# Prompt attention on one core: a stepped order, probabilities turned before they are divided by their sums

## The chip, the cores and the metric

One core of one Trainium2 chip. The metric is the device time of one execution in microseconds (us), as a median of several runs. A core has five engines that run side by side and wait for one another through semaphores: TensorE (PE, matmuls and transposes, its weight loads listed as PEld), VectorE (DVE), ScalarE (ACT), GpSimd (POOL), and SyncE (SP), which issues the DMA transfers here. SBUF is the working memory; PSUM, in banks of 128 x 512 float32, is where TensorE writes. GpSimd works on SBUF alone in this kernel.

## The reference

The program is one inference step of a two-layer trunk on 1024 prompt tokens and 8 x 8 sample tokens: an RWKV-7 layer, then a layer of sliding-window attention, each with a SiLU gate and an output projection. The part at stake is the prompt's attention of the second layer: 8 tiles of 128 queries, 16 heads of 64 in 4 groups that share keys and values, a window of 128, so each tile sees two blocks of 128 keys (the first tile one). All is float32.

```python
def window_attend(q, k, v, q_pos, k_pos, sinks):
    s = jnp.einsum('bnqhgd,bnshd->bnhgqs', q, k) * ATT_SCALE
    dist = q_pos[:, :, None] - k_pos[:, None, :]
    s = s - alibi_slopes()[None, None, :, :, None, None] * dist
    s = jnp.where(live, s, NEG)              # live: 0 <= dist < WINDOW
    p = softmax(concatenate([s, sink], -1))[..., :-1]
    return jnp.einsum('bnhgqs,bnshd->bnqhgd', p, v)

o = window_attend(...)                       # (tokens, 1024)
out = (o * silu(gate)) @ w_out
```

## The kernel before

The program runs its stages one after the other: mixed projections, the delta rule, a first output projection with layer norm, the attention's projections with the sample attention, the prompt attention (`attention`, L1862 on), and a second output projection with layer norm (`out2`, matmuls at L1434). A barrier stands between the last two, and the second needs all of `o`, the gated attention output. The order on each engine inside `attention` is written out by hand: each engine has its own loop over tiles `t` and head groups `g` and waits on counting semaphores.

For a group of four heads (`t`, `g`):
- TensorE `scores` (L1954) multiplies queries and keys into one of two PSUM tiles `sc`, two heads to a bank.
- VectorE `bias_group` (L2032) scales, adds the bias table and takes the maximum of each row (L2041, one operation a head), then makes `low`, the negative of the larger of maximum and sink, in two small operations (L2047, L2049), and `extra`, the sink less that maximum (L2051).
- ScalarE `raise_group` (L2005) takes the exponential in place with its row sum (L2009, one a head, each followed by a read of the accumulator), then that of `extra` (L2012).
- VectorE `norm_group` (L2053) adds `extra` to the sums and takes the reciprocal.
- GpSimd multiplies the probabilities of each head by the reciprocal of its sum (L1936), 128 x 256 at a time.
- TensorE `turn_probs` (L1942) transposes them into the two banks of `turn`, bank `s` for key block `s`; ScalarE `keep_probs` (L1997) copies both banks to `prob_t` in SBUF.
- TensorE `values` (L1964) multiplies values and probabilities of two groups into the PSUM tile `pv`, the two groups on the two halves of the partitions.
- VectorE `gate_group` (L2060) multiplies `pv` by the gate into `o`, four multiplies of 64 x 256 for two groups.

Scores and exponentials of tile `t` are mixed with the transposes and values of tile `t - 1`. At the end of each tile TensorE also transposes the values of the tile (L1988), through the first `turn` bank, and ScalarE copies them (L2023). SyncE loads for each tile `q_in`, the keys (four transfers, eight for tiles 4 and 7, whose preceding block is loaded again), `v_in` and `gate`; the load of tile `t`'s gate waits for the gating of tile `t - 2`, and the next tile's loads stand behind it.

Of the kernel before, what the change touches and what calls it, by code (L numbers as in the profile page):

```python
# [16 lines left out]
ALU = mybir.AluOpType  # L17
# [4 lines left out]
DT = D // 128  # L22
SEQ, NB, NT = 1024, 8, 8
N = SEQ + NB * NT
TILES = SEQ // 128
# [1836 lines left out]
def attention(nc, group, a, scr, outp, o, tables, o_sample, ahead):  # L1862
# [3 lines left out]

    with Tensors(nc, "att", group) as m:

        q_in, keys = m.sb("q_in", 128, 2, DT, 128), m.sb("keys", 128, KVH, 4 * 128)
        v_in, gate = m.sb("v_in", 128, 2, 2, 128), m.sb("gate", 128, 2, DT, 128)  # L1870
        v_rows = m.sb("v_rows", 128, 2, 256)
# [4 lines left out]
        top, low, sums, extra = (m.sb(x, 128, H) for x in ("top", "low", "sums", "extra"))  # L1876
# [6 lines left out]
        v_turned, v_kept = m.sem("v_turned"), m.sem("v_kept")  # L1883
        scored, biased, topped, lowered, sunk = (m.sem(x) for x in ("scored", "biased", "topped", "lowered", "sunk"))
        raised, totalled, inverted, normed = (m.sem(x) for x in ("raised", "totalled", "inverted", "normed"))
        p_turned, p_kept, mixed, gated = (m.sem(x) for x in ("p_turned", "p_kept", "mixed", "gated"))
# [11 lines left out]
        PLACE = (0, 1, 2, 3, 1, 2, 3, 1)  # L1898

        with nc.Block() as block:  # L1900
            @block.sync
            def _(sp):
# [27 lines left out]
            @block.gpsimd  # L1930
            def _(pool):
                for t in range(TILES):
                    for g in range(KVH):
                        pool.wait_ge(inverted, 4 * t + g + 1)
                        for h in range(4 * g, 4 * g + 4):
                            pool.tensor_scalar(score[:, t % 2, h, 0:width(t)], score[:, t % 2, h, 0:width(t)], sums[:, h:h + 1], None, ALU.mult).then_inc(normed, 1)  # L1936

            @block.tensor
            def _(pe):
                pe.wait_ge(small_loaded, 32)  # L1940

                def turn_probs(b, g):  # L1942

                    pe.wait_ge(normed, 16 * b + 4 * g + 4)
                    if b or g:
                        pe.wait_ge(p_kept, 4 * b + g)
                    if g == 0:
                        pe.wait_ge(v_kept, b + 1)
                    for s in range(len(blocks(b))):
                        for h in range(4):  # L1950
                            mm = pe.transpose(turn[:, s, 128 * h:128 * h + 128], score[:, b % 2, 4 * g + h, 128 * s:128 * s + 128], ident[:])
                    mm.then_inc(p_turned, 1)
# [11 lines left out]
                def values(b, i):  # L1964
                    pe.wait_ge(p_kept, 4 * b + 2 * i + 2)
                    if b:
                        pe.wait_ge(gated, 8 * (b - 1) + 4 * i + 4)
                    for s, k in enumerate(blocks(b)):
                        for e in range(2):
                            g = 2 * i + e  # L1970
                            mm = pe.matmul(pv[64 * e:64 * e + 64, i, :], v_rows[:, k % 2, 64 * g:64 * g + 64], prob_t[:, g, s, :],
                                           start=s == 0, stop=k == b)
                    mm.then_inc(mixed, 1)

                for t in range(TILES):
                    pe.wait_ge(loaded[t % 2], 32 * (t // 2 + 1))
                    pe.wait_ge(keys_loaded[t % 2], 64 * sum(2 if u and PLACE[u] <= PLACE[u - 1] else 1 for u in range(t % 2, t + 1, 2)))
                    for g in range(KVH):
                        if t:
                            turn_probs(t - 1, g)  # L1980
                        scores(t, g)
                        if t and g % 2:
                            values(t - 1, g // 2)
                    if t:

                        pe.wait_ge(p_kept, 4 * t)
                    for j in range(2):
                        mm = pe.transpose(turn[:, 0, 128 * j:128 * j + 128], v_in[:, t % 2, j, :], ident[:])  # L1988
                    mm.then_inc(v_turned, 1)
                for g in range(KVH):  # L1990
                    turn_probs(TILES - 1, g)
                    if g % 2:
                        values(TILES - 1, g // 2)

            @block.scalar
            def _(act):
                def keep_probs(b, g):  # L1997
                    act.wait_ge(p_turned, 4 * b + g + 1)
                    if b:
                        act.wait_ge(mixed, 2 * (b - 1) + g // 2 + 1)  # L2000
                    for s in range(len(blocks(b))):
                        keep = act.activation(prob_t[:, g, s, :], turn[:, s, :], ACT.Copy)
                    keep.then_inc(p_kept, 1)

                def raise_group(t, g):  # L2005

                    act.wait_ge(lowered, 4 * t + g + 1)
                    for h in range(4 * g, 4 * g + 4):
# [267 lines left out]
```

## Time and profile before

| | us |
|---|---|
| median of 3 runs | 1588.14 |
| lowest and highest | 1587.09, 1591.98 |
| the profiled execution, its own time | 1592.97 |
| its span | 1591.2 |
| prompt attention in it | 1337.1 to 1477.1 |
| second output projection in it | 1477.1 to 1591.2 |

The profile is one execution recorded by the hardware. "Busy" is the time in which an engine has at least one instruction under way; PE's matmuls overlap one another and their ends are modelled, so PE's busy time says less than the distance from one start to the next. PEclk is the granted TensorE clock as a share of 2.4 GHz; 0.50 is 1.2 GHz. A name such as `att_turn` is the program's tile `turn` of stage `att`.

### The profile page before, as it was taken

The page shows a single profiled execution, that of the slowest core. Times are in us where ns is not written, and L with a number is a line of the kernel's source. Part 1 is how long each engine was busy: PE and PEld are TensorE (multiplying, and loading weights), DVE is VectorE, ACT ScalarE, POOL GpSimd, SP SyncE. Part 2 cuts the span into 40 slices and gives each one's busy share as a digit, 9 for nine tenths or more (in the row PEclk, how much of TensorE's full clock was granted, in tenths as well). Part 3 has the DMA queues.
Part 4 walks back from the last instruction along what each step waited for, and adds up shares of the span by engine and source line. Part 5 has one row for each costly group of instructions (what it writes and reads, how often), then busy time and mean ns, then how long its engine had stood idle before and what let it go on. Part 6 is the DMA issues. An engine that isn't in the chain of part 4 may idle for free. (4 is left out here: it accounts for less than half of the span.)

```text
span 1591.2 us, 39091 instructions
## 1 busy us (share of the span) xinstructions
PE 1462.3 (92%) x16960; PEld 1305.3 (82%) x16960; DVE 821.4 (52%) x1662; ACT 594.1 (37%) x1207; POOL 307.5 (19%) x344
## 2 busy tenths in 40 slices
PE   5999999999699499999999978999999997887897
PEld 5989898888599499999999946889999995544686
DVE  6636345777610257776677544471111122886446
ACT  7526347777511022122221314251111132786424
POOL 0000000000000244455444420000001001997000
PEclk9999999999899699999999988999999998999899
DMA  6523222556541653345334127206334344331202
GB/s 219 180 61 91 83 96 88 174 174 212 156 135 43 141 134 72 82 96 149 87 73 90 37 67 260 79 1 204 85 82 120 83 125 130 124 98 39 81 27 86
DMA packets 242379, 173.56 MB, mean 109 GB/s; under 512 B 148607, under 2 KB 218175, under 8 KB 241039
## 3 DMA queue, kind: packets, MB, share of 16 engines
q1 hardware_dynamic: 209063, 155.56, 33.8%
q10 hardware_dynamic: 33152, 15.60, 3.3%
q8 instruction: 129, 2.11, 0.5%
q14 instruction: 35, 0.29, 0.1%
HBM read 110.97 MB, written 60.46 MB: 108 GB/s over the span
## 5 line engine op out<-in xcount | busy, mean ns | idle before, releaser
L329 PE MATMUL mix_acc<-mix_high,mix_w_high 128*128 128x364 f32 (+1 forms) x768 | 181.6, 345 | 19.4 <-DVE mix_w_low L543 13.9
L329 PE MATMUL mix_acc<-mix_low,mix_w_high 128*128 128x364 f32 (+1 forms) x768 | 172.0, 333 | 4.3 <-DVE mix_low L529 4.1
L329 PE MATMUL mix_acc<-mix_high,mix_w_low 128*128 128x364 f32 (+1 forms) x768 | 171.5, 332 | 0.0
L329 PEld LDWEIGHTS mix_acc<-mix_high,mix_w_high 128*128 128x128 f32 x768 | 132.2, 191 | 40.9 <-issue 20.7
L329 PEld LDWEIGHTS mix_acc<-mix_low,mix_w_high 128*128 128x128 f32 x768 | 134.6, 191 | 6.4 <-DVE mix_low L529 6.4
L329 PEld LDWEIGHTS mix_acc<-mix_high,mix_w_low 128*128 128x128 f32 x768 | 135.6, 191 | 0.0
L1936 POOL TENSOR_SCALAR att_score<-att_score,att_sums 128x256 f32<-128x256 f32 (+1 forms) x128 | 110.3, 882 | 119.4 <-DVE att_sums L2058 119.4
L543 DVE TENSOR_TENSOR mix_w_low<-mix_wt,mix_w_high 128x1024 fp32r<-128x1024 f32 x32 | 39.2, 1225 | 135.0 <-ACT mix_w_high L391 134.7
L1328 PE MATMUL out_acc<-qkvg_room_r_high,qkvg_room_w_high 128*128 128x364 f32 (+1 forms) x320 | 105.8, 331 | 3.0 <-issue 1.9
L1328 PE MATMUL out_acc<-qkvg_room_r_low,qkvg_room_w_high 128*128 128x364 f32 (+1 forms) x320 | 105.2, 329 | 0.0
L1328 PE MATMUL out_acc<-qkvg_room_r_high,qkvg_room_w_low 128*128 128x364 f32 (+1 forms) x320 | 105.2, 329 | 0.0
L405 ACT ACTIVATE mix_out<-mix_acc 128x364 f32<-128x364 f32 (+1 forms) x96 | 38.4, 473 | 168.9 <-PE mix_acc L329 168.8
L1638 DVE CAST qkvg_room_w_high<-qkvg_room_wt 128x1024 fp32r<-128x1024 f32 x20 | 14.0, 699 | 154.4 <-DMA qkvg_room_wt<-in_w_att 154.4
L925 PE MATMUL delta_gram<-delta_kr,delta_bk 64*64 64x128 f32 x1088 | 73.1, 282 | 21.9 <-DMA delta_seq_mask<-in_seq_mask 17.2
L1143 ACT ACTIVATE delta_lm<-delta_lm 128x128 f32<-128x128 f32 x96 | 26.5, 276 | 171.9 <-PE delta_lm L960 169.6
L925 PEld LDWEIGHTS delta_gram<-delta_kr,delta_bk 64*64 64x64 f32 x1088 | 62.9, 140 | 23.4 <-DMA delta_seq_mask<-in_seq_mask 17.5
L253 POOL MEMSET mix_decay<- 128x16 f32 x8 | 1.0, 128 | 395.6 <-ACT mix_decay L459 395.6
L524 DVE SCALAR_TENSOR_TENSOR early_xs<-early_xpad,mix_rest_mu,early_xs 128x1024 f32<-128x1024 f32 x96 | 68.7, 777 | 6.8 <-ACT early_xs L369 6.8
L1238 DVE TENSOR_TENSOR delta_inv<-delta_inv,delta_grown 128x256 f32<-128x256 f32 (+1 forms) x96 | 36.0, 375 | 68.4 <-PE delta_grown L975 68.4
L1203 DVE TENSOR_TENSOR delta_grams<-delta_gram,delta_gram_mask 128x512 f32<-128x512 f32 x68 | 44.6, 674 | 45.1 <-PE delta_gram L925 45.1
L2009 ACT ACTIVATE att_score<-att_score,att_low 128x256 f32<-128x256 f32 (+1 forms) x128 | 61.5, 487 | 8.9 <-DVE att_low L2049 8.7
L1685 ACT ACTIVATE qkvg_room_out<-out_acc 128x364 f32<-128x364 f32 (+1 forms) x40 | 18.7, 474 | 120.6 <-PE out_acc L1328 120.6
(253 smaller groups left out, 3495.8 us busy)
## 6 DMA issues: line engine op xcount, KB each, us to landing
mix_wt<-in_w_in SPq DMA_DIRECT2D x32, 512.0 KB, 4.1
qkvg_room_wt<-in_w_att SPq DMA_DIRECT2D x20, 512.0 KB, 4.1
delta_bk<-scr_bk SPq DMA_DIRECT2D x17, 512.0 KB, 4.6
delta_kr<-scr_kr SPq DMA_DIRECT2D x17, 512.0 KB, 7.0
scr_kr<-mix_outs SPq DMA_DIRECT2D x16, 512.0 KB, 3.5
scr_bk<-mix_outs SPq DMA_DIRECT2D x16, 512.0 KB, 4.4
early_xpad<-in_xpad SPq DMA_DIRECT2D x8, 548.5 KB, 8.2
scr_xg<-early_xs SPq DMA_DIRECT2D x8, 544.0 KB, 2.7
```

Source lines behind the costliest of these rows:

```text
L329: mm = pe.matmul(acc[:, s, k, 0:width], w[:, s, d, :], r[:, d, n0:n0 + width], start=d == 0 and q == 0, stop=d == DT - 1 and q == 2)
L405: act.activation(out[:, s, n0:n0 + width], acc[:, s, k, 0:width], ACT.Silu if n >= G_ * DT else ACT.Copy).then_inc(evacuated, 1)
L524: dve.scalar_tensor_tensor(o[k], x[k], rest_mu[:, place, d:d + 1], o[k], ALU.mult, ALU.add).then_inc(mixed, 1)
L543: dve.tensor_tensor(w_low[:, n % 2], wt[:, n % 2], w_high[:, n % 2].bitcast(F32), ALU.subtract).then_inc(w_split, 1)
L925: mm = pe.matmul(gram_bank[n % 2][p, 256 * j + 128 * k:256 * j + 128 * k + 128], bk[p, c % 2, k, pair, :], kr[p, c % 4, :, pair, :], start ...
L1143: act.activation(blocks(lm[:, lev, 4 * g:4 * g + 4, :].rearrange("p j n -> p (j n)"), lev, 0), lm_bank[g][:, 0:128].rearrange("p (m b) -> ...
L1203: dve.tensor_tensor(grams[:, c % 3, 2 * n:2 * n + 2], gram_bank[n % 2][:, :].rearrange("p (j k n) -> p j k n", j=2, k=4), mask, ALU.mult). ...
L1238: dve.tensor_tensor(dst, dst, src, ALU.add).then_inc(grown_kept, 1)
L1328: mm = pe.matmul(out, w[:, d, :], r[:, d, columns], start=d == 0 and k == 0, stop=d == DT - 1 and k == 2)
L1685: act.activation(out[:, s, n0:n0 + n], banks[s][k][:, 0:n], ACT.Silu if name == "ag" else ACT.Copy).then_inc(evacuated, 1)
L1936: pool.tensor_scalar(score[:, t % 2, h, 0:width(t)], score[:, t % 2, h, 0:width(t)], sums[:, h:h + 1], None, ALU.mult).then_inc(normed, 1)
L2009: act.activation(score[:, t % 2, h, 0:width(t)], score[:, t % 2, h, 0:width(t)], ACT.Exp, bias=low[:, h:h + 1], accum_out=sums[:, h:h + 1] ...
```

## The change

The order becomes steps. `STEPS` counts `n` from -1 to 36; group `n` is tile `n // 4`, head group `n % 4`, and in step `n` each engine does its part for a fixed lag: TensorE the scores of group `n + 1`, the transposes of group `n - 3` and, in odd steps, the values of a pair of groups; VectorE the bias of group `n`, the reciprocal of group `n - 2`; ScalarE the exponentials of group `n - 1` and the evacuation of group `n - 3`.

The probabilities are no longer divided by their sums. Instead the reciprocals are spread: in even steps GpSimd copies those of 8 heads 64 times each into `wide` (128 x 512), as the first thing in its step, TensorE transposes `wide` into a `turn` bank (`spread_sums`), and VectorE multiplies the gate by it in place (`scale_gate`). `gate_half` then multiplies `pv` and gate in one 128 x 512 operation for two groups; for this `values` writes pairs of heads to the two partition halves, by 256 columns. GpSimd also adds the sink terms. VectorE evacuates the second block of odd groups (`by_vector`). The `turn` banks are used in the order of the list `USES`, alternating. All values are loaded in one transfer and transposed in step 2.

```diff
+        USES = [("values", k) for k in range(TILES // 2)]
+        for tile in range(TILES):
+            for group4 in range(KVH):
+                if group4 % 2 == 1:
+                    USES.append(("sums", tile, group4 // 2))
+                USES += [("probs", tile, group4, part) for part in range(len(blocks(tile)))]
+        def by_vector(b, g, s):
+            return g % 2 == 1 and s == 1
+        def turn_bank(*use):
+            return turn[:, USES.index(use) % 2, :]
+        STEPS = range(-1, GROUPS + 5)
...
             @block.sync
                     if t >= 2:
                         sp.wait_ge(scored, 4 * (t - 1))
-                        sp.wait_ge(v_turned, t - 1)
...
-                    sp.dma_start(v_in[:, slot], scr["av"][t]).then_inc(loaded[slot], 16)
+                    if t == 0:
+                        sp.dma_start(v_in[:], scr["av"][0:TILES].rearrange("t p j n -> p t j n")).then_inc(v_loaded, 16)
                     if t >= 2:
-                        sp.wait_ge(gated, 8 * (t - 1))
+                        sp.wait_ge(gated, 2 * (t - 1))
                     sp.dma_start(gate[:, slot], scr["ag"][t]).then_inc(gate_loaded[slot], 16)
...
             @block.gpsimd
-                            pool.tensor_scalar(score[:, t % 2, h, 0:width(t)], score[:, t % 2, h, 0:width(t)], sums[:, h:h + 1], None, ALU.mult).then_inc(normed, 1)
+                pool.tensor_scalar(less_sink[:], sink[:], -1.0, None, ALU.mult).then_inc(sink_turned, 1)
...
+                    pool.wait_ge(lowered, n + 1)
+                    pool.tensor_tensor(extra[:, hs], low[:, hs], sink[:, hs], ALU.add).then_inc(sunk, 1)
...
+                    pool.wait_ge(raised, 5 * n + 5)
+                    pool.tensor_tensor(total, total, extra[:, 4 * g:4 * g + 4], ALU.add).then_inc(totalled, 1)
...
+                def widen(b, i):
+                    pool.wait_ge(inverted, 4 * b + 2 * i + 2)
+                    if b:
+                        pool.wait_ge(spread, 2 * (b - 1) + i + 1)
+                    rows = sums[:, b % 2, 8 * i:8 * i + 8].rearrange("p (h o) -> p h o", o=1).broadcast_to([128, 8, 64])
+                    pool.tensor_copy(wide[:, i, :].rearrange("p (h n) -> p h n", h=8), rows).then_inc(widened, 1)
+                for n in STEPS:
+                    if live(n - 3) and n % 2 == 0:
+                        widen((n - 3) // 4, (n - 3) % 4 // 2)
+                    if live(n):
+                        add_sink(n)
+                    if live(n - 1):
+                        total_sums(n - 1)
...
             @block.tensor
+                def spread_sums(b, i):
+                    pe.wait_ge(widened, 2 * b + i + 1)
+                    wait_for_bank("sums", b, i)
+                    for j in range(4):
+                        mm = pe.transpose(turn_bank("sums", b, i)[:, 128 * j:128 * j + 128], wide[:, i, 128 * j:128 * j + 128], ident[:])
+                    mm.then_inc(spread, 1)
...
+                    for g in (2 * i, 2 * i + 1):
+                        for s, k in enumerate(blocks(b)):
+                            probs = prob_t[:, g, s, :].rearrange("p (j h n) -> p h j n", j=2, h=2)
+                            for h in range(2):
+                                at = 256 * (g % 2)
+                                mm = pe.matmul(pv[64 * h:64 * h + 64, i, at:at + 256], v_rows[:, k, 64 * g:64 * g + 64], probs[:, h], start=s == 0, stop=k == b)
...
+                for n in STEPS:
+                    if live(n + 1):
+                        scores(t, (n + 1) % 4)
+                    if n == 2:
+                        pe.wait_ge(v_loaded, 16)
+                        for k in range(TILES // 2):
+                            turn_values(k)
+                    if live(n - 5) and n % 2 == 1:
+                        values((n - 5) // 4, (n - 5) % 4 // 2)
+                    if live(n - 3):
+                        if n % 2 == 0:
+                            spread_sums((n - 3) // 4, (n - 3) % 4 // 2)
+                        turn_probs((n - 3) // 4, (n - 3) % 4)
...
             @block.scalar
+                for n in STEPS:
+                    if live(n - 1):
+                        raise_group((n - 1) // 4, (n - 1) % 4)
+                    if n == 2:
+                        for k in range(TILES // 2):
+                            act.wait_ge(v_turned, k + 1)
+                            act.activation(v_rows[:, 2 * k:2 * k + 2, :].rearrange("p t n -> p (t n)"), turn_bank("values", k), ACT.Copy).then_inc(v_kept, 1)
+                    if live(n - 3):
+                        keep_probs((n - 3) // 4, (n - 3) % 4)
...
             @block.vector
+                    dve.scalar_tensor_tensor(low[:, hs], top[:, hs], -1.0, less_sink[:, hs], ALU.mult, ALU.min).then_inc(lowered, 1)
...
+                for n in STEPS:
+                    if live(n):
+                        bias_group(n // 4, n % 4)
+                    if live(n - 2):
+                        invert_sums(n - 2)
+                    if live(n - 3) and n % 2 == 0:
+                        scale_gate((n - 3) // 4, (n - 3) % 4 // 2)
+                        if n - 3 >= KVH:
+                            keep_probs((n - 3) // 4, (n - 3) % 4)
+                    if live(n - 5) and n % 2 == 1:
+                        gate_half((n - 5) // 4, (n - 5) % 4 // 2)
```

`wait_for_bank` waits until the use of `turn` two places back in `USES` has been read: by ScalarE for values and most blocks, by VectorE for sums (`gate_scaled`) and the blocks of `by_vector` (`p_kept_too`). `keep_probs` (VectorE) is the copy of such a block to `prob_t`.

## Rows read from the trace of the kernel before

**Rows 1.** Stretches: length, busy PE PEld DVE ACT POOL (count), PEclk, DMA, GB/s.
```profile
1342.50:1356.10 13.60, 10.31 (x60) 7.29 (x60) 8.79 (x62) 8.10 (x39) 8.56 (x15) 0.54 1.00 351
...
1401.40:1416.60 15.20, 12.65 (x84) 7.35 (x82) 13.50 (x60) 12.61 (x46) 14.60 (x17) 1.00 0.33 101
...
1459.20:1477.10 17.90, 11.05 (x40) 4.86 (x40) 3.72 (x10) 4.30 (x9) 5.96 (x7) 0.71 0.00 0
1477.10:1591.20 114.10, 102.22 (x432) 82.54 (x432) 57.51 (x79) 42.15 (x71) 0.10 (x1) 0.94 0.18 68
```

**Rows 2.** Waits, 1325 to 1480: total us, times, longest.
```profile
POOL att_score L1936 <- DVE att_sums L2058: 119.4, 11, 112.1
...
PEld att_turn L1951 <- POOL att_score L1936: 19.1, 21, 2.2
```

**Rows 3.** Timeline, steady part: start, length, engine, line, op, count [idle before].
```profile
1408.68 14.41 POOL L1936 TENSOR_SCALAR att_score<-att_score,att_sums 128x256 f32<-128x256 f32 x16 [0.60 <-DVE att_sums L2058]
...
1408.68 1.94 PE L1971 MATMUL att_pv<-att_prob_t,att_v_rows 128*64 128x512 f32 x8 [0.79 <-ACT att_prob_t L2002]
...
1410.55 0.44 PE L1988 MATMUL att_turn<-all_ident,att_v_in 128*128 128x128 f32 x2
...
1411.56 1.07 PE L1951 MATMUL att_turn<-all_ident,att_score 128*128 128x128 f32 x8 [0.57 <-ACT att_v_rows L2023]
...
1412.55 1.14 PE L1960 MATMUL att_sc<-att_keys,att_q_in 64*128 64x256 f32 x8
...
1413.90 0.42 DVE L2041 CUSTOM_DVE_ANT_0 att_score<-att_sc,all_bias 128x256 f32<-128x256 f32 x1
...
1415.41 0.16 DVE L2047 TENSOR_TENSOR att_low<-att_top,all_sink 128x4 f32<-128x4 f32 x1
...
1415.67 1.08 ACT L2002 ACTIVATE att_prob_t<-att_turn 128x512 f32<-128x512 f32 x2 [1.25 <-PE att_turn L1951]
...
1416.64 0.51 ACT L2009 ACTIVATE att_score<-att_score,att_low 128x256 f32<-128x256 f32 x1
...
1417.13 0.50 ACT L2009 ACTIVATE att_score<-att_score,att_low 128x256 f32<-128x256 f32 x1
...
1425.83 0.44 PE L1988 MATMUL att_turn<-all_ident,att_v_in 128*128 128x128 f32 x2
```

**Rows 4.** Timeline, change from tile 0 to tile 1.
```profile
1350.91 0.71 PEld L1951 LDWEIGHTS att_turn<-all_ident,att_score 128*128 128x128 f32 x4 [3.12 <-issue]
...
1356.12 0.51 ACT L2009 ACTIVATE att_score<-att_score,att_low 128x256 f32<-128x256 f32 x1 [0.41 <-DVE att_low L2049]
```

**Rows 5.** Groups by shape, GpSimd and VectorE: count | busy, mean ns | idle before.
```profile
L902 POOL TENSOR_TENSOR delta_below<-delta_grams,delta_level_mask 128x512 f32<-128x512 f32 x48 | 59.6, 1270 | 0.0
...
L1203 DVE TENSOR_TENSOR delta_grams<-delta_gram,delta_gram_mask 128x512 f32<-128x512 f32 x68 | 44.6, 674 | 45.1 <-PE delta_gram L925 45.1
...
L551 DVE COPY early_v_tokens<-mix_acc 128x512 f32<-128x512 f32 x16 | 10.3, 685 | 23.4 <-PE mix_acc L267 23.4
```

**Rows 6.** Two small VectorE lines: count, ns least/median/most, first and last start.
```profile
L2047 DVE TENSOR_TENSOR att_low<-att_top,all_sink x32: 161/163/553, 1344.9 to 1455.6; 128x4 f32<-128x4 f32 x32
...
L2049 DVE TENSOR_SCALAR att_low<-att_low x32: 169/354/508, 1345.1 to 1455.8; 128x4 f32<-128x4 f32 x32
```

**Rows 7.** Timeline, end of prompt attention.
```profile
1459.09 0.19 ACT L2012 ACTIVATE att_extra<-att_extra 128x4 f32<-128x4 f32 x1
...
1471.75 3.30 PE L1971 MATMUL att_pv<-att_prob_t,att_v_rows 128*64 128x512 f32 x8 [1.18 <-ACT att_prob_t L2002]
...
1475.10 1.78 DVE L2067 TENSOR_TENSOR all_o<-att_pv,att_gate 64x256 f32<-64x256 f32 x4 [6.47 <-PE att_pv L1971]
```

**Rows 8.** SyncE's issues for tile 7, and landing times of all key loads.
```profile
1428.06 0.33 SPq L1921 DMA_DIRECT2D att_gate<-scr_ag  x1
...
1428.91 5.04 SPq L1907 DMA_DIRECT2D att_keys<-scr_ak  x8
...
DMA to landing us min/median/max: 2.2/3.7/8.5
```

More of the change, by code:

```diff
@@ L1875, in attention @@
         gate_sample = m.sb("gate_sample", 128, DT, NB * NT)
-        top, low, sums, extra = (m.sb(x, 128, H) for x in ("top", "low", "sums", "extra"))
+        top, low, extra, less_sink = (m.sb(x, 128, H) for x in ("top", "low", "extra", "less_sink"))
+        sums, wide = m.sb("sums", 128, 2, H), m.sb("wide", 128, 2, 512)
         sc = m.ps("sc", 128, 2, 2, 512)
@@ L1882, in attention @@
         gate_loaded = [m.sem(f"gate_loaded{i}") for i in range(2)]
[L1883 to L1886, printed above, removed]
+        v_loaded, v_turned, v_kept = m.sem("v_loaded"), m.sem("v_turned"), m.sem("v_kept")
+        scored, biased, lowered, sunk, sink_turned = (m.sem(x) for x in ("scored", "biased", "lowered", "sunk", "sink_turned"))
+        raised, totalled, inverted = (m.sem(x) for x in ("raised", "totalled", "inverted"))
+        widened, spread, gate_scaled = m.sem("widened"), m.sem("spread"), m.sem("gate_scaled")
+        p_turned, p_kept, p_kept_too, mixed, gated = (m.sem(x) for x in ("p_turned", "p_kept", "p_kept_too", "mixed", "gated"))
         copied, own_loaded = m.sem("copied"), m.sem("own_loaded")
@@ L1964, in values @@
                 def values(b, i):
-                    pe.wait_ge(p_kept, 4 * b + 2 * i + 2)
+                    pe.wait_ge(p_kept, 1 + max(PROBS_ACT.index(use) for use in PROBS_ACT if use[1:3] == (b, 2 * i + 1)))
                     if b:
[L1967 to L1972, printed above, removed]
@@ L1973, in values @@
-                    mm.then_inc(mixed, 1)
[L1975 to L1989, printed above, removed]
@@ L2025, in _ @@
-                for g in range(KVH):
-                    keep_probs(TILES - 1, g)
+                for n in STEPS:
[7 more added lines that the diff above has]
+                        keep_probs((n - 3) // 4, (n - 3) % 4)
@@ L2045, in bias_group @@
                     if t:
-                        dve.wait_ge(normed, 16 * (t - 1) + 4 * g + 4)
-                    dve.tensor_tensor(low[:, hs], top[:, hs], sink[:, hs], ALU.max).then_inc(topped, 1)
-                    dve.wait_ge(topped, 4 * t + g + 1)
-                    dve.tensor_scalar(low[:, hs], low[:, hs], -1.0, None, ALU.mult).then_inc(lowered, 1)
-                    dve.wait_ge(lowered, 4 * t + g + 1)
-                    dve.tensor_tensor(extra[:, hs], low[:, hs], sink[:, hs], ALU.add).then_inc(sunk, 1)
@@ L2069, in _ @@
[L2069 to L2081 removed]
+                        dve.wait_ge(raised, 5 * (4 * t + g - 4) + 5)
@@ new lines, in scale_gate, with gate_half @@
+                def scale_gate(b, i):
+                    if i == 0:
+                        dve.wait_ge(gate_loaded[b % 2], 16 * (b // 2 + 1))
+                    dve.wait_ge(spread, 2 * b + i + 1)
+                    half = gate[:, b % 2, 4 * i:4 * i + 4, :]
+                    dve.tensor_tensor(half, half, turn_bank("sums", b, i).rearrange("p (j n) -> p j n", j=4), ALU.mult).then_inc(gate_scaled, 1)
+                def gate_half(b, i):
+                    dve.wait_ge(mixed, 2 * b + i + 1)
+                    dve.wait_ge(gate_scaled, 2 * b + i + 1)
+                    dve.tensor_tensor(o[:, 4 * i:4 * i + 4, 128 * b:128 * b + 128], pv[:, i, :].rearrange("p (j n) -> p j n", j=4),
+                                      gate[:, b % 2, 4 * i:4 * i + 4, :], ALU.mult).then_inc(gated, 1)
@@ L2082, in _ @@
                         dve.wait_ge(own_loaded, 16)
                         dve.tensor_tensor(o[:, :, SEQ:N], o_sample[:], gate_sample[:], ALU.mult).then_inc(own_gated, 1)
-                for g in range(KVH):
-                    gate_group(TILES - 1, g)
 _INS = {
```

125 lines of the change are left out of this document (66 added, 59 removed).

## Prediction

> **What bounds the kernel now.** I read the stretches first [rows 1]. Prompt attention lies between 1337.1 and 1477.1 us; the last stretch, the output projection with 102.2 us of matmul in 114.1 us, is not touched. In the 15.2 us from 1401.4, one tile of attention, GpSimd is busy 14.6 us, VectorE 13.5, PE 12.65 (modelled), ScalarE 12.6. The waits [rows 2] say who sets the beat: GpSimd waits for the reciprocals 119.4 us in all, but 112.1 of that ahead of its first instruction, while the transposes wait 19.1 us for GpSimd. The timeline of a tile [rows 3] agrees: the 16 scalings of one tile run from 1408.68 as a block of 14.41 us (0.90 each) after a stall of 0.60, and the values' transposes come at 1410.55 and 1425.83, 15.28 us apart. GpSimd bounds now, the others are some 2 us behind. The end is a second loss: the last exponential group ends at 1459.3 and the last gating at 1476.9 [rows 7], 17.6 us in which the engines take turns. The granted clock there is a mean 0.71 [rows 1], and the last values pass takes 3.30 us [rows 7] where 1.94 is usual [rows 3]: the level of 1.2 GHz, after PE had stood idle.
>
> **What goes.** All 128 scalings of the probabilities; 96 of 160 four-column VectorE operations (`topped`, and `sunk` and `totalled`, which GpSimd gets); 64 half-height gate multiplies; 14 of the 60 evacuations of ScalarE (VectorE gets them); the load and the transposition of values inside each tile.
>
> **What comes, by engine, for two steps (half a tile, 8 heads).** Durations are start to start.
> PE: a block is half of the 8 transposes from 1411.56 to 1412.55, with its wait 0.47 us; a scores call 1.03 (the 1.14 of [rows 3] less an overlap of 0.1); values 1.87 (1408.68 to 1410.55). The new values call splits each 512-column matmul into two of 256, the same columns, so 1.87 again. Two scores, one values, four blocks and one spread of sums, each spread like a block: 2.06 + 1.87 + 1.88 + 0.47 = 6.3 us.
> ScalarE: an exponential with its sum is 0.49 (1416.64 to 1417.13), an evacuation 0.48 (two from 1415.67 to 1416.64). A group with the sink's 0.10 is 2.06. Two groups and three evacuations: 5.6 us.
> VectorE: four bias operations up to the first low operation take 1.51 (1413.90 to 1415.41); the one scalar_tensor_tensor in place of three small ones 0.2 and the reciprocal 0.2: 1.9 a step. `keep_probs` is a copy of 128x512 out of PSUM: 0.69 [rows 5]. `scale_gate` and `gate_half` multiply that shape, one operand in PSUM: 0.67 [rows 5], taken as 0.69. Sum 3.8 + 2.07 = 5.9 us.
> GpSimd: no row has a copy from a broadcast source of 128x512. Bounds: nothing on the path if hidden, and 1.80 (twice the 0.90 of 256 scaled columns); two-input work of the shape is 1.27 [rows 5], and a copy reads half of that, so 1.1. With four small adds of some 0.25: 2.1 us, far from bounding.
> No engine alone needs more than 6.3 us where half a tile takes 7.64 now.
>
> **The loop that bounds after.** The blocks and the spread sums alternate over the two `turn` banks in one list, so the block (odd g, s=1) must wait until VectorE has used the sums in its bank. Take the start of the spread as 0. Four transposes are readable after 0.68 (pitch 0.11 and a last one of 0.27, which make the 1.07 of eight [rows 3]; 0.04 to wake the reader); `scale_gate` ends at 1.37; the second block is then transposed and readable at 2.09; VectorE copies it until 2.78; values hold PE from 2.83 to 4.70; two blocks to 5.64; scores to 6.67; then the next spread. The pair's other scores fit in PE's wait from 1.84 to 2.83. On VectorE the same turn is 2.78 + 1.9, a wait to 4.8 for the values, 0.69, and 1.9: 7.4, and the next `scale_gate` is due 6.7 after this one at 0.68. Both close at 6.7 us. ScalarE has kept its blocks by 2.4 and 6.45; GpSimd's widening runs from 4.7 to 5.8 and is needed at 6.7. Both are hidden, with 0.4 and 0.9 us to spare; a widening of 1.80 would end at 6.5. If the cover is gone, each us of it is a us in each pair, 14 in all. So half a tile costs 6.7 instead of 7.64.
>
> **Start.** The first scores no longer wait for the values' load (under 1 us), but 16 transposes and four ScalarE copies now stand between the third and fourth step. At the clock there, mean 0.54 [rows 1], four transposes take 0.71 of weight loads [rows 4], and copies of 0.59 alternate with them over two banks; this holds ScalarE some 3 us. By the same bookkeeping the first group of tile 1 starts at 1356.6, where now it starts at 1356.1 [rows 4]. What tile 0 no longer waits for GpSimd is given back. The 0.9 MB of values that now go ahead of tile 1's q and keys are 2.6 us at the 351 GB/s of that stretch [rows 1]; the transposes cover them.
>
> **Sum.** Tile 1's first group at 1356.6; two steps of 2.6 and one of 3.2 while tile 0's single blocks drain, so the eighth group starts at 1365.0; 24 more at 3.35: the last starts at 1445.4 and ends at 1447.5 (now 1459.3). Drain, by the steps above: reciprocal 0.5, then the turning, `scale_gate`, second block, `keep_probs`, values, `gate_half` of the last pair, held up by the pair ahead of it: 8.3 us, and 1.4 for a values pass at the low clock (3.30 less 1.94): 1457.2. I add 1.2 for hand-offs that a chain on paper leaves out: 1458.4 against 1476.9. Saving 18.5 us: 11.8 before the last exponential, 7.9 from the drain, less the addition. Profiled execution: 1593.0 less 18.5 is 1574.5; it lies 4.8 above the median of the runs (1588.1), so 1569.7, rounded to 1570.
>
> **Steps costed at nothing.** Key loads: in tiles 4 and 7 the eight take SyncE 5.04 us, from 0.85 after the gate's issue, and land 2.2 to 3.7 later (least and median) [rows 8]. Afterwards the gate's issue comes when VectorE ends step 4t-5, and the keys are due at PE's step 4t-1, 9.8 us later by the loop; 0.85 + 5.04 + 2.2 to 3.7 is 8.1 to 9.6. Hidden, barely; at the worst landing of 8.5, nearly 5 us in one of the two tiles. The tiles with four loads have 2.5 us more. The `less_sink` operation comes ahead of any scores.
>
> **One port.** While GpSimd streams, VectorE's one-input low operation has a median of 0.354 us against a least of 0.169, the two-input one ahead of it 0.163 against 0.161 [rows 6]. These are partial delays at most, and 1.1 us of widening in 6.7 meets few of them, so none is in the sum. The Trainium skill (SBUF — State Buffer, Who interferes with whom) says that a GpSimd instruction that reads SBUF blocks a VectorE instruction with two SBUF inputs until it ends. By that rule the new low operation could lose up to one widening. The rows here show less.
>
> **Rivals.**
> 1. The loop does not close at 6.7: a late evacuation or widening delays the blocks behind it in the two-bank order, or the widening holds up the low operation, 1.1 us in each of 14 pairs at most. For: three engines hand over within each pair. Against: 0.4 and 0.9 us of slack. At 7.2 to 7.64 a pair it gives back 7 to 13 us: 1577 to 1583. Chance 0.20.
> 2. PE's 6.3 us is the pair and the drain runs at the full clock: 14 x 0.4 and 1.4 less, 1563. For: the issue counts. Against: the bank wait is in the code. Chance 0.12.
> 3. PE falls to the lower clock in the steady part. PE's 6.3 become 12.6, 5.9 more in each such pair: from four of 14 on the kernel is slower than before, and all 14 give 1653. For: 0.54 in the first stretch, 0.71 in the drain. Against: 1.00 in the tile shown [rows 1], and PE's gaps shrink. Chance 0.07. The Trainium skill (TensorE: Matmul & The Clock Gate, Part 4: PE-mode transpose) says that transposes do not count as PE activity for the clock; the change adds 64 of them, and by that rule they would not help to hold it. The other matmuls are 3.9 us of each pair, now in 7.64, then in 6.7.
> 4. Another engine at once takes 15 us a tile and the drain's gain is lost in the new start: within 0.3%. Chance 0.05.
> The forecast, 1565 to 1577, has the remaining 0.56.
>
> **Numbers.** 0.3% is 4.8 us, about what this kernel's runs can tell. Faster (under 1583.4): 0.56 + 0.12 + 0.20, less 0.01 for rival 1's edge, 0.87; same 0.05; slower 0.07 + 0.01. The range takes in rivals 1 and 2: 1561 to 1582.
>
> **What would show it.** Right: 6.6 to 6.9 us from values to values; GpSimd busy under 5 us a tile with the widening at 1.0 to 1.3; VectorE waiting some 0.7 us for the second block of each pair; the last exponential near 1447, the last gating near 1458. Wrong: transposes that wait for the widened sums, ScalarE without idle time, a granted clock under 1.00 in the steady part, scores of tiles 4 and 7 that wait for keys. The likeliest error is small waits: 0.3 us more in each pair is 4 us.

## The result and the profile after

The changed kernel takes 1574.58 us (median of 5 runs, 1571.64 to 1577.46), the kernel before 1588.14 (1587.07 to 1604.3): ratio 0.9889, 95% interval 0.9840 to 0.9939. Forecast were 1570 and 1561 to 1582. The profiled execution took 1574.79 us, span 1573.0; the one before 1592.97 and 1591.2, so 18.2 us less (18.5 forecast). The medians are only 13.6 us apart where 18.1 were forecast.

The start of prompt attention moves by some us between executions, whatever its kernel (1332.3 to 1340.2 in the traces here), so I compare the stage's own length: from SyncE's first load of `q_in` to GpSimd's first operation behind the stage. Before 1337.12 to 1477.17, 140.05 us; after 1336.92 to 1460.02, 123.10. These lengths come from one trace each; the same kernel traced once more (**e6**) gave 123.26. What lies ahead is the same within 0.2 us. The output projection takes 113.0 us instead of 114.1, but 114.2 in e6, so this 1.1 us is chance: 16.95 of the 18.2 us belong to the stage. The stretches after, same columns as [rows 1]:

```profile
1341.80:1354.60 12.80, 12.01 (x82) 9.64 (x84) 7.40 (x50) 9.67 (x43) 2.31 (x10) 0.71 1.05 367
1399.10:1406.20 7.10, 6.76 (x55) 4.59 (x53) 5.36 (x25) 5.72 (x23) 1.31 (x5) 1.00 0.06 6
1450.30:1460.00 9.70, 6.69 (x52) 4.63 (x52) 3.30 (x6) 2.15 (x4) 0.82 (x2) 1.00 0.00 0
1460.00:1573.00 113.00, 101.17 (x432) 81.75 (x432) 57.44 (x79) 42.16 (x71) 0.10 (x1) 0.96 0.18 69
```

Half a tile (7.1 us) has 6.76 us of PE in it, and GpSimd, busy 14.60 of 15.2 us in [rows 1], now 1.31 of 7.1. PE in one half tile:

```profile
1406.18 0.66 PE L2021 MATMUL att_turn<-all_ident,att_wide 128*128 128x128 f32 x4
1406.67 0.60 PE L2029 MATMUL att_turn<-all_ident,att_score 128*128 128x128 f32 x4
1407.69 0.66 PE L2029 MATMUL att_turn<-all_ident,att_score 128*128 128x128 f32 x4 [0.41 <-DVE att_gate L2145]
1408.28 1.13 PE L2038 MATMUL att_sc<-att_keys,att_q_in 64*128 64x256 f32 x8
1409.34 1.95 PE L2054 MATMUL att_pv<-att_prob_t,att_v_rows 128*64 128x256 f32 x16
1411.22 1.09 PE L2029 MATMUL att_turn<-all_ident,att_score 128*128 128x128 f32 x8
1412.24 1.13 PE L2038 MATMUL att_sc<-att_keys,att_q_in 64*128 64x256 f32 x8
1413.31 0.65 PE L2021 MATMUL att_turn<-all_ident,att_wide 128*128 128x128 f32 x4
```

From one spread (L2021) to the next are 7.13 us; the values alternate 7.05 and 7.12 apart (1402.21, 1409.34, 1416.39), 7.09 in the mean. PE has one real stop, the 0.41 us (0.34 in the other halves) ahead of the second block, until `scale_gate` (L2145) has freed the bank of the sums. VectorE's copy of that block is over at 1409.07, before PE comes to the values at 1409.34:

```profile
1406.94 0.69 DVE L2145 TENSOR_TENSOR att_gate<-att_gate,att_turn 128x512 f32<-128x512 f32 x1 [0.39 <-PE att_turn L2021]
...
1408.38 0.69 DVE L2138 COPY att_prob_t<-att_turn 128x512 f32<-128x512 f32 x1 [0.75 <-PE att_turn L2029]
```

The waits of the stage (total, times, longest) and the widening:

```profile
ACT att_prob_t L2083 <- PE att_turn L2029: 20.5, 15, 2.7
DVE att_prob_t L2138 <- PE att_turn L2029: 10.5, 14, 0.8
...
PE att_turn L2029 <- DVE att_gate L2145: 5.2, 14, 0.4
...
PEld att_turn L2021 <- POOL att_wide L1980: 1.2, 2, 0.9
```

```profile
L1980 POOL COPY att_wide<-att_sums 128x512 f32<-128x512 f32 x16 | 9.8, 616 | 0.3 <-DVE att_sums L2133 0.3
```

The bank wait comes in all 14 half tiles, the wait for widened sums in two, and no score of tile 4 or 7 waits for keys.

### The profile page after: what moved, and what is told of

Same layout as the page of the kernel before. It is cut to its first block and busy times, and to the rows that moved or that the text cites. A ratio compares the mean times of both kernels' runs of the same rounds, so it can differ in the third digit from the quotient of the medians.

```text
span 1573.0 us, 39379 instructions
## 1 busy us (share of the span) xinstructions
PE 1463.7 (93%) x17144; PEld 1321.4 (84%) x17144; DVE 798.0 (51%) x1548; ACT 586.2 (37%) x1189; POOL 219.1 (14%) x297
## 5 line engine op out<-in xcount | busy, mean ns | idle before, releaser
L1328 PEld LDWEIGHTS out_acc<-qkvg_room_r_high,qkvg_room_w_high 128*128 128x128 f32 x320 | 60.7, 190 | 3.4 <-issue 3.4
L1328 PEld LDWEIGHTS out_acc<-qkvg_room_r_low,qkvg_room_w_high 128*128 128x128 f32 x320 | 60.8, 190 | 0.0
```

What stands on the lines that cost most here:

```text
L1328: mm = pe.matmul(out, w[:, d, :], r[:, d, columns], start=d == 0 and k == 0, stop=d == DT - 1 and k == 2)
```

## Experiments

All ratios are against the kernel before, run on the same chip; its median there was 1593.8 us for e1 to e4 and 1592.4 for e5 to e12, some 4 to 6 us above the first line. So ratios are to be compared, not medians, and a difference of 0.003 between two ratios is within their intervals. The stage length, from one trace each, tells more. The half tile is the distance of the values' starts in the steady part, mean of neighbours where they alternate.

| run | stage us | half tile us | median us | ratio (95%) |
|---|---|---|---|---|
| before | 140.05 | 7.64 | 1588.14 | |
| after | 123.10 | 7.09 | 1574.58 | 0.9889 (0.984 to 0.9939) |
| e1 spread late | 121.43 | 6.89 | 1576.42 | 0.9886 (0.9852 to 0.992) |
| e2 ScalarE keeps all | 123.31 | 7.09 | 1580.43 | 0.9919 (0.989 to 0.9948) |
| e3 no spread | 113.64 | 6.24 | 1567.48 | 0.9839 (0.98 to 0.9878) |
| e4 widening last | 187.92 | 10.6 to 12.3 | 1638.49 | 1.0273 (1.0233 to 1.0313) |
| e5 late spread, VectorE first | 117.71 | 6.64 | 1568.49 | 0.9847 (0.9816 to 0.9877) |
| e6 after again | 123.26 | 7.09 | 1575.94 | 0.9888 (0.9861 to 0.9914) |
| e7 steps, scaled | 139.24 | 7.83 | 1591.69 | 0.9990 (0.9968 to 1.0013) |
| e8 old order, little scaling | 139.93 | 7.64 | 1593.31 | 0.9995 (0.997 to 1.0021) |
| e9 old order, no scaling | 140.30 | 7.64 | 1590.53 | 0.9987 (0.9956 to 1.0018) |
| e10 widening three times | 126.48 | 7.09 | 1579.63 | 0.9900 (0.9843 to 0.9956) |
| e11 old, by block, no scaling | 128.64 | 7.12 | 1580.45 | 0.9923 (0.9894 to 0.9953) |
| e12 old, by block | 130.41 | 7.20 | 1580.35 | 0.9923 (0.9895 to 0.9951) |

### What the new half tile is made of (e1, e2, e3, e5)

**e1** moves the spread and `scale_gate` to the odd step, ahead of the values:

```
 if live(n - 5) and n % 2 == 1:
+    spread_sums((n - 5) // 4, (n - 5) % 4 // 2)
     values((n - 5) // 4, (n - 5) % 4 // 2)
 if live(n - 3):
-    if n % 2 == 0:
-        spread_sums((n - 3) // 4, (n - 3) % 4 // 2)
     turn_probs((n - 3) // 4, (n - 3) % 4)
```

> The spread of the sums is moved on TensorE from ahead of the probability transposes of an even step to ahead of the values of the next odd step; its multiply on VectorE moves with it, ahead of gate_half. Nothing is left out. Theory A: half a tile is TensorE's own issue, about 6.7 us, plus a wait of 0.34 to 0.41 us for scale_gate, because the second probability block needs the bank of the sums. With the wait gone the pair falls from 7.09 to 6.7 to 6.8, the kernel by 4 to 6 us: 1569 to 1571. Theory B: VectorE's chain of operations and waits sets the pair; its work is the same, so the pair stays at 7.0 to 7.1 and the time at 1573 to 1576.

Half tile 6.89, between the two theories, and a stage 1.7 us shorter; the ratio does not tell it from the changed kernel. The wait got smaller and changed its place: the spread now waits for an evacuation by ScalarE, which comes behind its exponentials.

```profile
1404.65 0.63 PE L2021 MATMUL att_turn<-all_ident,att_wide 128*128 128x128 f32 x4 [0.21 <-ACT att_prob_t L2082]
```

**e2** gives VectorE's 14 evacuations back to ScalarE:

```
-    return g % 2 == 1 and s == 1
+    return False
```

> ScalarE evacuates all probability blocks again; VectorE loses 14 copies of 0.69 us and its waits of 0.75 us for them. Nothing is left out. Theory A (TensorE with its bank wait): the bank wait and TensorE's issue are unchanged, ScalarE has 1.4 us idle in each pair and takes 0.48 more, so the time stays within 2 us of 1574.6. Theory B (VectorE's chain): 0.7 to 1.4 us less in each of 14 pairs, 1555 to 1565. Third possibility: ScalarE's exponentials get in front of the block that values wait for, 0.3 to 0.5 us more a pair, 1579 to 1582.

Half tile and stage as in the changed kernel: VectorE's turn does not set the beat. The median, 1580.43, lies in the range of the third possibility, but its half tile did not come; the kernel before was 5.6 us slower on this chip too.

**e3** leaves out the division by the sums: no widening, no spread, no `scale_gate`.

> Leaves out the division by the sums: no widening, no spread transposes, no scale_gate. Reciprocals are still taken. Theory A: each pair loses the spread's 0.49 us of TensorE and the bank wait of 0.38, so 6.2 us a pair and 12 us less in 14 pairs, with 1 to 2 us in the drain: 1560 to 1562. Theory B: each pair loses VectorE's 0.69 and its wait of 0.3 to 0.4: 1 us a pair, 1559; the two are told apart by whether TensorE or VectorE still has idle time. If the spreading were hidden altogether, 1574.

Half tile 6.24, and PE has 12.25 us of work in one tile of 12.48:

```profile
1400.00:1412.48 12.48, 12.25 (x98) 8.31 (x97) 9.26 (x44) 11.36 (x43) 1.60 (x9) 1.00 0.34 106
```

So without spread and bank wait PE's issue of blocks, scores and values is 6.24, where my count had 5.81. The half tile is theory A's; the stage is only 9.5 us shorter, not 12, because the saving was counted for 14 pairs, and in the changed kernel only ten of the 15 distances between values are the 7.05 and 7.12 of the steady part. The others are 5.49 to 6.89.

**e5** is e1 with two copies traded: of the odd groups VectorE keeps the first block, ScalarE the second.

```
-    return g % 2 == 1 and s == 1
+    return b > 0 and g % 2 == 1 and s == 0
```

> Order of the run with the late spread, and the two copies of the odd steps trade engines: VectorE keeps the first block's, ScalarE the second's. Theory (TensorE's wait of 0.2 to 0.4 us a pair is for a bank whose copy comes late): the bank that the spread needs is then free before it, the wait goes, and a pair takes 6.55 to 6.7 us instead of 6.89 and 7.09; the attention stage 117 to 119 us instead of 121.4 and 123.1, and the time 1567 to 1571 against 1574.6. Rival (TensorE's wait is only passed on, since ScalarE's exponentials or VectorE's gating now end last): pair 6.9 to 7.1, time 1573 to 1577.

```profile
1398.08 1.95 PE L2054 MATMUL att_pv<-att_prob_t,att_v_rows 128*64 128x256 f32 x16
1399.96 1.09 PE L2029 MATMUL att_turn<-all_ident,att_score 128*128 128x128 f32 x8
1400.98 1.13 PE L2038 MATMUL att_sc<-att_keys,att_q_in 64*128 64x256 f32 x8
1402.05 1.09 PE L2029 MATMUL att_turn<-all_ident,att_score 128*128 128x128 f32 x8
1403.07 1.13 PE L2038 MATMUL att_sc<-att_keys,att_q_in 64*128 64x256 f32 x8
1404.13 0.66 PE L2021 MATMUL att_turn<-all_ident,att_wide 128*128 128x128 f32 x4
```

The timeline of PE shows no stop between the calls: 1.88 + 1.02 + 1.07 + 1.02 + 1.06 + 0.59 = 6.64 us from values to values. That is PE's own time for this work, and the bank wait of the changed kernel is the rest of its 7.09. This version leaves nothing out. Its stage is 5.6 us shorter than the changed kernel's, and it takes 1568.49 us (1567.39 to 1575.86) beside 1575.94 (1573.87 to 1580.69) for the changed kernel (**e6**) on the same chip: four of its five runs lie below all six of e6, while the intervals of the two ratios still touch.

> The changed kernel again, on the same chip as its variants. Both theories: 1572 to 1578 us, ratio 0.986 to 0.992, attention stage 123 us, pair 7.05 to 7.12.

### What the widening costs (e4, e10)

**e4** puts the widening behind the two small operations of its step on GpSimd.

```
-if live(n - 3) and n % 2 == 0:
-    widen((n - 3) // 4, (n - 3) % 4 // 2)
 if live(n):
     add_sink(n)
 if live(n - 1):
     total_sums(n - 1)
+if live(n - 3) and n % 2 == 0:
+    widen((n - 3) // 4, (n - 3) % 4 // 2)
```

> GpSimd's widening comes last in its step, behind the sink's addition and the totalling of the sums, which waits for ScalarE's exponentials of the step. Nothing is left out. In the profile after, the widening ends 1.7 us before the spread; placed last it starts when the group's exponentials are done, some 4.3 us later, so the spread waits about 2.6 us. Theory A with this on its path: 9.0 to 9.7 us a pair, 1601 to 1611, slower than the kernel before. If the order on GpSimd does not matter, 1574.

The half tile grows by about twice what was expected: 4.4 us in the mean instead of 1.9 to 2.6. Three lines of PE's timeline:

```profile
1413.69 0.66 PE L2021 MATMUL att_turn<-all_ident,att_wide 128*128 128x128 f32 x4 [2.54 <-POOL att_wide L1980]
...
1416.24 2.08 PE L2038 MATMUL att_sc<-att_keys,att_q_in 64*128 64x256 f32 x8
1418.25 3.49 PE L2054 MATMUL att_pv<-att_prob_t,att_v_rows 128*64 128x256 f32 x16
```

The widening now stands behind the sums of a later group, so the spread comes 2.5 us late; after each such stop the scores take 2.08 us instead of 1.13 and the values 3.49 instead of 1.95, the level of 1.2 GHz. Over 1360 to 1500 the granted clock is a mean 0.80. The wait of 2.5 us and the slow stretch behind it make the half tile 10.6 to 12.3 us, 3.5 to 5.2 more than 7.09. I had priced the wait alone.

**e10** leaves the order and widens three times over, each copy waiting for the one ahead.

```
+for k in range(2):
+    pool.tensor_copy(wide[:, i, :]...).then_inc(again, 1)
+    pool.wait_ge(again, 2 * (2 * b + i) + k + 1)
 pool.tensor_copy(wide[:, i, :]...).then_inc(widened, 1)
```

> The changed kernel with each widening of the sums done three times over (the same values; nothing left out), so some 1.9 us on GpSimd instead of 0.62. Theory (it begins at about 1403.9 and the spread needs it at 1406.2, 2.3 us later, and nothing else on GpSimd is due before): hidden, half tile 7.05 to 7.15 us, stage 123 to 124 us, time 1573 to 1578. Rival (the waits it passes on add up, or VectorE's small operations with two inputs in SBUF wait behind it): half tile 7.4 or more, stage 128 or more, time 1580 or more.

The theory was right for the steady part, where 1.9 us of widening are hidden: half tile 7.09. But the stage is 3.4 us longer, about 2.8 of it in the fill (the first tiles) and 0.6 in the drain (the last steps), where less slack is left than the 2.3 us that I had taken everywhere. The rival's stage of 128 us and more did not come either. The first spreads of this run:

```profile
1355.03 0.66 PE L2025 MATMUL att_turn<-all_ident,att_wide 128*128 128x128 f32 x4 [1.54 <-POOL att_wide L1984]
...
1361.05 0.66 PE L2025 MATMUL att_turn<-all_ident,att_wide 128*128 128x128 f32 x4 [1.19 <-POOL att_wide L1984]
...
1367.06 0.66 PE L2025 MATMUL att_turn<-all_ident,att_wide 128*128 128x128 f32 x4 [0.75 <-POOL att_wide L1984]
```

VectorE's small operation with two inputs in SBUF kept its mean (166 ns, 174 in the changed kernel).

### Which part of the change brings the gain (e7, e8, e9, e11, e12)

**e7** keeps the order in steps and scales the probabilities on GpSimd as before, with transposes and values one step later; widening, spread and `scale_gate` go. **e8** is the kernel before, with the scaling cut to 4 of up to 256 columns (most of the division is left out):

```
 # e7
 pool.wait_ge(inverted, n + 1)
 for h in range(4 * g, 4 * g + 4):
     pool.tensor_scalar(score[:, t % 2, h, 0:width(t)], score[:, t % 2, h, 0:width(t)], sums[:, t % 2, h:h + 1], None, ALU.mult)
 # e8
-pool.tensor_scalar(score[:, t % 2, h, 0:width(t)], score[:, t % 2, h, 0:width(t)], ...)
+pool.tensor_scalar(score[:, t % 2, h, 0:4], score[:, t % 2, h, 0:4], ...)
```

> The two-step order with GpSimd scaling the probabilities as before, the spreading of the sums left away; nothing of the computation left out. Theory (the gain comes from taking the scaling off GpSimd, whose 16 scalings of 0.90 us and 8 small adds of 0.2 make 16 us a tile): half tile 8.0 to 8.5 us, stage 140 to 147 us, time 1588 to 1600, no faster than before. Rival (the order in steps is the gain, the unscaled probabilities only move work about): half tile 7.0 to 7.2, stage about 123, time about 1574.

> The kernel before with GpSimd's scaling cut to 4 of the 256 columns of each head (most of the division by the sums is left out): the old order with GpSimd all but free, without the two-step order and without a spread. Theory (the order in steps only lets TensorE go on where GpSimd's work is gone; by busy time alone VectorE's 13.3 us a tile and TensorE's 12.6 would do): half tile 6.6 to 7.0 us, stage 121 to 128, time 1570 to 1577. Rival (the old order itself makes TensorE wait for exponentials in a row): half tile 7.3 to 7.64, stage 134 to 140, time 1582 to 1588.

Neither half of the change brings a gain that can be told alone. In e7 GpSimd works without a pause, 15.6 us a tile; it is the bound (half tile 7.83, a little under the theory's range):

```profile
1409.68:1425.30 15.62, 12.24 (x98) 8.29 (x96) 9.43 (x47) 12.76 (x46) 15.62 (x25) 1.00 0.28 85
```

e7 is no clean test of the order: the eight small adds a tile that the new order gives to GpSimd are 1.2 of these 15.6 us. Scaling alone would be 14.4; steps with scaling and without these adds were not run.

In e8, with GpSimd nearly free, the half tile stays at 7.64. The theory is wrong; half tile and stage are at the upper edge of the rival's ranges. **e9** takes the scaling out altogether (the division is left out); the transposes wait for the exponentials.

> The kernel before without GpSimd's scaling at all: the transposes wait for the exponentials themselves (the division by the sums is left out). With the scaling cut to four columns the half tile stayed at 7.64 us, and there each group's transposes began 1.1 us after the last exponential of the group (sums, reciprocal, the first scalings), while ScalarE, which comes to the evacuations before the next exponentials, stood for 1.0 to 1.25 us twice a half tile. Theory (the old order is a loop in series: exponentials, sums, scaling, transposes, evacuations): taking the two hand-overs out shortens the half tile to 6.7 to 7.0 us, where VectorE's 6.65 is next; stage 124 to 130 us, time 1575 to 1582. Rival (another loop of the old order, the values with the two-column-block gating behind them, sets 7.64): half tile 7.5 to 7.64, time 1588 to 1594.

The theory missed again: 7.64. The rival's number came, but it named another loop than the one found. Without GpSimd the timeline of PE and of ScalarE's evacuations shows what is left:

```profile
1400.36 1.06 ACT L1998 ACTIVATE att_prob_t<-att_turn 128x512 f32<-128x512 f32 x2
...
1401.56 1.06 PE L1947 MATMUL att_turn<-all_ident,att_score 128*128 128x128 f32 x8 [0.88 <-ACT att_prob_t L1998]
...
1402.66 1.08 ACT L1998 ACTIVATE att_prob_t<-att_turn 128x512 f32<-128x512 f32 x2 [1.25 <-PE att_turn L1947]
...
1403.80 1.94 PE L1967 MATMUL att_pv<-att_prob_t,att_v_rows 128*64 128x512 f32 x8
```

PE waits for ScalarE to empty both banks, ScalarE then for PE to fill both. ScalarE's 1.25 us and PE's 0.79 ahead of the values are to the digit those in [rows 3], with GpSimd at work. **e11** and **e12** therefore hand the two banks over one by one, in e9 and in the kernel before; not one operation is added or moved.

```
-if b or g:
-    pe.wait_ge(p_kept, 4 * b + g)
 for s in range(len(blocks(b))):
+    pe.wait_ge(p_kept, ...)          # the last copy out of bank s
     for h in range(4):
         mm = pe.transpose(turn[:, s, ...], ...)
-mm.then_inc(p_turned, 1)
+    mm.then_inc(p_turned, 1)
 ...
 for s in range(len(blocks(b))):
+    act.wait_ge(p_turned, ...)       # bank s is filled
-    keep = act.activation(prob_t[:, g, s, :], turn[:, s, :], ACT.Copy)
-keep.then_inc(p_kept, 1)
+    act.activation(prob_t[:, g, s, :], turn[:, s, :], ACT.Copy).then_inc(p_kept, 1)
```

> The run without scaling (old order, the division left out), and the two transpose banks handed over one by one: TensorE and ScalarE signal each 128-row block instead of each pair, with no operation added or moved. Without GpSimd the half tile had stayed at 7.64 us, with ScalarE waiting 1.25 and 1.0 us a tile-half for pairs of transposed blocks and TensorE 0.9 and 0.8 for the evacuations of pairs. Theory (that give and take of a pair of banks between TensorE and ScalarE is the second loop of 7.64 us): it loses 0.5 to 1.0 us a half tile, 6.7 to 7.1; stage 126 to 132 us, time 1577 to 1584. Rival (another loop): 7.5 to 7.64, time 1588 to 1594.

> The kernel before, with the scaling, and the transpose banks handed over one by one; nothing left out. Theory (the old order has two loops of 15.28 us a tile, and GpSimd's 16 scalings of 0.90 us with their stall of 0.6 are the other): half tile 7.4 to 7.64 us, stage 137 to 140, time 1587 to 1593, no gain that can be told. Rival (GpSimd's work was never a bound): it falls with the run without scaling, to 7.1 or less, time 1577 to 1585.

The theory of the pair of banks holds: against the kernel before the stage is 11.4 us shorter in e11 and 9.6 in e12, and both ratios are clear of 1. My forecast for e12 was wrong; its time fell as the rival said, and its half tile of 7.20 lies between the two. Its tile is 14.39 us (values at 1413.47 and 1427.86), and in it GpSimd has no idle time:

```profile
1413.47:1427.86 14.39, 12.67 (x84) 7.35 (x82) 13.56 (x61) 13.05 (x45) 14.39 (x17) 1.00 0.31 106
```

GpSimd's bound is 16 x 0.90 = 14.4 us a tile, not the 15.28 of the kernel before: the stall of 0.60 us in each tile [rows 3] was not GpSimd's, it was the other loop showing through. e11, without GpSimd, closes at 14.24; what bounds it there was not looked into.

## Why the prediction was right, and where it was not

**"GpSimd bounds now, the others are some 2 us behind": wrong.** This step failed. What set 15.28 us a tile was PE and ScalarE passing a pair of banks to and fro; GpSimd's 14.4 lay only 0.9 behind. e9 shows it, since nothing changes when GpSimd's work is gone, and e12, since the hand-over alone brings 9.6 us of the stage. The 19.1 us of transposes waiting for GpSimd [rows 2] were real but free: GpSimd came last by a little. The misreading did not spoil the total, because the time was added up from the steps of the new kernel and the old bound is in none of its terms. That the change removes the real bound too was luck: it hands blocks over singly, which the prediction counts nowhere as a gain, besides emptying GpSimd and staggering the groups. Of 17 us of stage, 9.6 can be had by the first alone; from e12's 130.41 to 123.10 are the other two together. The two were not separated further with the hand-over in place. The errors behind the total cancel in part: the loop lost 4.5 us before the last exponential group, the start gave 1.8 back, and the drain was 1.4 shorter.

**The loop of 6.7 a half tile: half right, and mis-sized, 7.09.** The wait for the bank of the sums is there as forecast. Behind it the path is another. In us from the spread's start, in the half tile shown above:

| | forecast | measured |
|---|---|---|
| `scale_gate` begins | 0.68 | 0.76 |
| second block begins | 1.41 | 1.51 |
| VectorE's copy of it ends | 2.78 | 2.89 |
| values begin | 2.83 | 3.16 |
| the next two blocks begin | 4.70 | 5.04 |
| second scores begin | 5.64 | 6.06 |
| next spread | 6.67 | 7.13 |

The forecast let the values wait for VectorE's copy, with a scores call in that wait. The scores call does stand there (1408.28), but it fills the time and more: the copy is done 0.27 us before the values begin, and PE does not stop. So behind the bank wait PE's own calls set the half tile, and e2, which takes the copy from VectorE, changes nothing. PE's calls were the short term: 6.3 forecast, 6.64 in e5, mostly blocks, 0.51 each within a pair and 0.59 for a single one or e5's spread instead of 0.47, and 1.07 for scores instead of 1.03. Part of that was a slip: the 0.99 us from 1411.56 to 1412.55 make 0.50 for a block, not 0.47. The pair lies between the forecast (6.9 at most) and rival 1 (7.2 at least). Between the starts of the eighth and the last exponential group are 84.9 us (1363.23 to 1448.12), forecast 80.4: 4.5 lost, of which 1.8 had come back by the eighth group, so the last exponential group is 2.8 late.

**Start: forecast 1356.6 for tile 1's first exponential, it was 1354.59.** Every PE call of the start was priced at the lower level of the clock. The scores at 1349.71 took 1.14 us, as at the full one; I put the 2.0 us down to this, and no run changes the clock alone. Granted clock, last column but two, in two stretches of the kernel after, and last in the kernel before over the same time:

```profile
1345.00:1349.00 4.00, 4.00 (x24) 3.32 (x22) 2.67 (x23) 3.81 (x18) 0.95 (x5) 0.50 1.08 368
1349.00:1351.00 2.00, 2.00 (x16) 1.43 (x15) 0.10 (x1) 1.62 (x5) 0.00 (x0) 0.96 1.35 388
```

```profile
1346.50:1350.50 4.00, 1.69 (x10) 1.06 (x10) 3.53 (x27) 3.88 (x23) 2.96 (x6) 0.50 1.04 325
1350.50:1354.50 4.00, 3.56 (x15) 2.44 (x16) 1.31 (x9) 2.41 (x12) 4.00 (x7) 0.50 0.98 408
```

After, PE works without a gap from 1345 to 1349, from 1346.38 on with the 16 transposes of values, and the clock then rises from 1.2 to 2.4 GHz; before, PE is busy 1.69 of four us and the clock is still low at 1354.5. e5 shows the same with less else in it, the transposes alone from 1344.02 on and the clock low until then:

```profile
1344.02 3.56 PE L2014 MATMUL att_turn<-all_ident,att_v_in 128*128 128x128 f32 x16
```

```profile
1344.00:1347.10 3.10, 3.10 (x16) 2.71 (x15) 1.43 (x14) 2.49 (x12) 0.56 (x4) 0.50 1.10 319
1347.50:1349.50 2.00, 1.91 (x15) 1.37 (x16) 0.66 (x3) 2.00 (x9) 0.00 (x0) 1.00 1.30 367
```

The Trainium skill (TensorE: Matmul & The Clock Gate, Part 4: PE-mode transpose) says that transposes do not count as PE activity. These two traces speak against it for such fp32 transposes, though scores ran just ahead of them in both. They are not the only way up: in e3 the clock rose before the first of them, behind scores.

**Drain: 8.3 us and 1.4 for the low clock, measured 9.5.** The last exponential group ended at 1450.28 (forecast 1447.5), the last gating at 1459.74 (1458.4). The clock stayed at 1.00 and the values took 1.95 us, so the 1.4 did not come, and the paper chain was short by 1.2, which is the addition made for hand-offs. Part of rival 2 came true, without its PE bound. That the output projection begins with a clock of 0.79 in its first 8 us, against 0.57, and is 1.1 us shorter is not the change's doing: in e6, the same kernel, it begins with 0.57 and takes 114.2 us:

```profile
1458.40:1466.40 8.00, 5.80 (x14) 4.16 (x15) 5.82 (x9) 7.95 (x12) 0.10 (x1) 0.57 0.01 2
1458.40:1572.60 114.20, 102.32 (x432) 82.64 (x432) 57.51 (x79) 42.14 (x71) 0.10 (x1) 0.94 0.18 68
```

Without this chance the profiled execution would have been some 17 us faster than the one before, not 18.2.

**Costed at nothing.** Keys: right. The widening: 0.616 us, forecast 1.1, bounds 0 and 1.80; hidden, but e10 shows that a widening of 1.9 would not be in fill and drain. The port: the 32 `low` operations have a mean of 174 ns, so there is next to nothing in the sum. One of them starts while the widening streams:

```profile
1352.30 0.61 POOL L1980 COPY att_wide<-att_sums 128x512 f32<-128x512 f32 x1
1352.40 0.53 DVE L2128 SCALAR_TENSOR_TENSOR att_low<-att_top,att_less_sink 128x4 f32<-128x4 f32 x1
```

It takes 0.53 us instead of 0.16, up to the widening's end at 1352.91. By the rule of the Trainium skill (SBUF — State Buffer, Who interferes with whom) it is blocked until GpSimd's instruction ends. This one case agrees, and in the steady part the two do not meet. The kernel before mostly disagrees: the two-input `low` operation at 1415.41 took 0.16 us in the middle of GpSimd's block of multiplies [rows 3], and of the 29 that began while such a multiply was under way, 23 took under 0.19.

**VectorE's work:** its copies (692 ns) and `scale_gate` (686) were priced right; the move of 14 copies off ScalarE brought nothing that the stage shows (e2, 123.31 against 123.10).

## What to carry to other kernels

An engine that is busy 96% of a stretch, with others waiting for it, need not be its bound, though it can be the next one, here 0.9 us a tile behind: take its work away and see, and be wary of a second loop whose waits (here 1.25 and 0.79 us, in both directions between two engines) repeat each round. Two engines that pass a pair of buffers as one unit alternate; a semaphore for each buffer costs no operation and alone brought 9.6 of the 17 us of this stage. A slack found in the steady part does not hold in fill and drain, and on PE a wait is to be priced with the slow clock that can follow it.

## What the hardware showed that I had not expected

With one stop of 2.5 us in each half tile the granted clock fell in every round (e4), and the half tile was 3.5 to 5.2 us longer; with one of 0.4 us (after), or with stops of 0.2 to 0.9 us (e9), it stayed at 1.00 in the steady part. It rose from 0.50 to 1.00 while PE did nothing but fp32 transposes (e5, from 1344.02). A copy of 128x512 from a broadcast 128x8 on GpSimd takes 0.616 us, less than half of the 1.27 of a two-input operation of that shape [rows 5].
